# Ten value tiles and six feature tiles moved between the last blocks of the first modulation, five of its blocks left unsplit

## What is computed

```python
mod = silu(cond) @ w_mod + b_mod            # shift1, scale1, gate1, shift2, scale2, gate2
h   = x * (1 + scale1) + shift1
z   = h @ w_in                              # q, k, v of 8 heads, and the latents of the second attention
# ... two attentions, w_o, layer norm
x   = layernorm(alpha * x + gate1 * o)
x   = layernorm(alpha * x + gate2 * swiglu(x * (1 + scale2) + shift2))
```

## Time and profile before

| | us |
|---|---|
| median of 3 runs (2892.14 to 2893.25) | 2892.49 |
| the profiled execution | 2892.7 |
| its span in the trace | 2891.1 |
| first modulation: first matmul, start of block 63 on PE | 7.73, 91.50 |
| first matmul of value block 0 | 99.62 |
| first matmul behind the value blocks | 215.12 |

### The profile page before, as it was taken

One profiled execution on the slowest core, in us unless ns is written; L12 is line 12 of the kernel. 1 busy time (PEld: TensorE's weight loads), 2 busy tenths in 40 slices (PEclk: granted clock), 3 DMA queues, 4 the chain that ended last, 5 costly groups with the idle time before them and its releaser, 6 DMA issues.

```text
span 2891.1 us, 42097 instructions
## 1 busy us (share of the span) xinstructions
PE 2814.6 (97%) x15844; PEld 2494.9 (86%) x15844; DVE 1889.6 (65%) x2939; ACT 1043.8 (36%) x1814; POOL 187.9 (6%) x262
## 2 busy tenths in 40 slices
PE   7899999999999999799999999999999999999996
PEld 2679999877888776799999999999999888888885
DVE  8766666585885787866666666666666555424337
ACT  7422333224453213644444444444444312112121
POOL 1121111000001000000000000000000000000005
PEclk9999999999999999899999999999999999999998
DMA  9754333352334655122222222222222535223231
GB/s 383 274 186 154 125 128 132 122 191 71 104 110 173 220 175 182 63 101 97 101 101 101 99 98 101 101 99 92 96 101 101 198 119 174 80 89 137 80 124 73
DMA packets 105768, 379.82 MB, mean 131 GB/s; under 512 B 14062, under 2 KB 14466, under 8 KB 103754
## 3 DMA queue, kind: packets, MB, share of 16 engines
q1 hardware_dynamic: 89088, 317.36, 30.9%
q0 software_dynamic: 16000, 61.06, 6.0%
q10 hardware_dynamic: 586, 0.12, 0.0%
HBM read 346.97 MB, written 33.48 MB: 132 GB/s over the span
## 4 chain that ended last, share of the span: by engine, by line
PE 90%; DVE 4%; DMA 2%; ACT 2%; issue 1%; SPq 0%; ACTq 0%; DVEq 0%
PE ps L1955 16%; PE ps L1957 16%; PE ps L1956 16%; PE ps L2455 12%; PE ps L2453 12%; PE ps L2454 12%; DMA mraw<-in_wstream 2%; PE ps L2154 1%; PE ps L2119 1%; DVE ps L1883 1%; PE ps L2102 1%; DVE acc L1885 1%; DVE stat L1933 0%; PE ps L2150 0%; PE ps L2093 0%
## 5 line engine op out<-in xcount | busy, mean ns | idle before, releaser
L2453 PE MATMUL ps<-actl,ringh 128*128 128x320 f32 x1408 | 435.5, 309 | 3.9 <-DVE ringl L1754 3.9
L2454 PE MATMUL ps<-acth,ringh 128*128 128x320 f32 x1408 | 435.1, 309 | 0.0
L2455 PE MATMUL ps<-actl,ringl 128*128 128x320 f32 x1408 | 435.1, 309 | 0.0
L2453 PE MATMUL ps<-acth,ringh 128*128 128x320 f32 x1056 | 327.1, 310 | 7.6 <-DVE ringl L1754 7.6
L2454 PE MATMUL ps<-actl,ringh 128*128 128x320 f32 x1056 | 326.9, 310 | 0.0
L2455 PE MATMUL ps<-acth,ringl 128*128 128x320 f32 x1056 | 326.8, 309 | 0.0
L1955 PE MATMUL ps<-dwh,fring 128*128 128x512 f32 x820 | 319.4, 390 | 1.0 <-DVE dwl L1858 1.0
L1957 PE MATMUL ps<-dwh,fring 128*128 128x512 f32 x820 | 319.2, 389 | 0.0
L1956 PE MATMUL ps<-dwl,fring 128*128 128x512 f32 x820 | 319.1, 389 | 0.0
L1858 DVE TENSOR_TENSOR dwl<-raw,dwh 128x1024 fp32r<-128x1024 f32 x82 | 100.4, 1224 | 291.4 <-ACT dwh L1319 291.4
L1754 DVE TENSOR_TENSOR ringl<-raw,ringh 128x512 fp32r<-128x512 f32 x264 | 181.7, 689 | 162.8 <-ACT ringh L1253 162.8
(11 more groups left out here) (310 smaller groups left out, 5775.0 us busy)
## 6 DMA issues: line engine op xcount, KB each, us to landing
raw<-in_wstream SPq DMA_DIRECT2D x503, 512.0 KB, 3.3
mraw<-in_wstream SPq DMA_DIRECT2D x64, 512.0 KB, 7.7
fscr<-fst POOLq DMA_DIRECT2D x44, 320.0 KB, 2.4
fst<-fscr SPq DMA_DIRECT2D x21, 640.0 KB, 4.1
acc<-in_xT SPq DMA_DIRECT2D x8, 640.0 KB, 16.0
oscr<-ost POOLq DMA_DIRECT2D x16, 320.0 KB, 2.5
ostage<-oscr POOLq DMA_DIRECT2D x16, 320.0 KB, 3.9
acc<-in_xtok POOLq DMA_DIRECT2D x4, 1280.0 KB, 7.4
```

The lines of the kernel that those rows point to most:

```text
L2453: mm(out, ringh[:, s, w], ah, start=first, stop=False, skip_group_check=True)
L2454: mm(out, ringh[:, s, w], al, start=False, stop=False, skip_group_check=True)
L2455: ins = mm(out, ringl[:, s, w], ah, start=False, stop=last, skip_group_check=True)
```

## The change

Between the last blocks of the modulation PE now computes value blocks 0 and 1, one value tile (six matmuls) behind each of the blocks 49, 50, 52, 54, 55 and 57, 58, 60, 62, 63. For this the feature tiles 0 to 5 are made between the splits of ACT and DVE, behind the blocks 43, 45, 48, 51, 56 and 60 (`H_AT`), value blocks 0 to 2 are split behind 47, 53 and 59 (`V_SPLIT`), and `mod1` is made in three parts. SP loads x 0, 1, 2 behind the blocks 36, 42 and 50 (`X_LOAD`) and the value blocks 0 to 3 behind 39, 46, 54 and 61 (`V_LOAD`). The blocks 44, 46, 50, 54 and 58 (`DIRECT`) aren't split: PE multiplies them as they are, with both operands in plain float32, in two matmuls in place of four. `modrow` has one buffer in place of two, the loops over the blocks are written out, and `mraw` and a few small buffers lie elsewhere in SBUF, so that feature tiles 0 to 5 don't overlap the blocks that are still in use. The product of block 2 is behind block 63, with the last `turn_rows` behind its first tile. What follows value block 2 is in the order of before.

The core of the diff:

```diff
+DIRECT = [44, 46, 50, 54, 58]
+SPLIT = [j for j in range(B_V) if j not in DIRECT]
+X_LOAD = {36: 0, 42: 1, 50: 2}
+V_LOAD = {39: 0, 46: 1, 54: 2, 61: 3}
+V_SPLIT = {47: 0, 53: 1, 59: 2}
+V_TILES = {49 + 8 * v + x: (v, t) for v in range(2) for t, x in enumerate((0, 1, 3, 5, 6))}
+H_AT = {43: 0, 45: 1, 48: 2, 51: 3, 56: 4, 60: 5}
+def mod_row(j):
+    return j
+def pe_order():
+    order = []
+    for j in range(B_V):
+        order.append(mod_row(j))
+        if j in V_TILES and V_TILES[j][1] == 4:
+            order.append(B_V + V_TILES[j][0])
+    return order
+PE_ORDER = pe_order()
...
+SPLITS = [n for k, n in ORDER if k == "w"]
+RAWS = [(k, n) for k, n in ORDER if k == "m" or n >= B_V]
+RAW_POS = {x: B_V + p for p, x in enumerate(RAWS)}
+RAW_END = B_V + len(RAWS)
...
-        MOD_BANKS = [7, 5]
+        MOD_BANKS = [4, 5]
...
-            for n in range(8):
-                sp.dma_start(mraw[:, n, :], wstream[n]).then_inc(mod_loaded[n], 16)
-            with sp.Fori(1, B_V // 8) as i:
-                for s in range(8):
-                    sp.wait_ge(lo_ready, i * 8 + (s - 7))
-                    sp.dma_start(mraw[:, s, :], wstream[i * 8 + s]).then_inc(mod_loaded[s], 16)
-            for g in range(8):
+            def mod_load(j):
+                if j - 8 in DIRECT:
+                    sp.wait_ge(used, used_count(mod_row(j - 8)))
+                elif j >= 8:
+                    sp.wait_ge(lo_ready, POS[("w", mod_row(j - 8))] + 1)
+                sp.dma_start(mraw[j % 8], wstream[mod_row(j)]).then_inc(mod_loaded[j % 8], 16)
+            def stream_load(p):
+                if p >= B_V + 4:
+                    sp.wait_ge(lo_ready, POS[RAWS[p - 4 - B_V]] + 1)
+                sp.dma_start(raw[:, p % 4, :], wstream[stream_row(p)]).then_inc(loaded[p % 4], 16)
+            for j in range(B_V):
+                mod_load(j)
+                if j in X_LOAD:
+                    g = X_LOAD[j]
+                    sp.dma_start(xstage[:, 2 * g:2 * g + 2, :], xT[:, 2 * g:2 * g + 2, :]).then_inc(x_in[g], 16)
+                if j in V_LOAD:
+                    stream_load(B_V + V_LOAD[j])
+            for g in range(3, 8):
                 sp.dma_start(xstage[:, 2 * g:2 * g + 2, :], xT[:, 2 * g:2 * g + 2, :]).then_inc(x_in[g], 16)
-                if g < 4:
-                    sp.dma_start(raw[:, g, :], wstream[stream_row(B_V + g)]).then_inc(loaded[g], 16)
-            def stream_load(p):
-                sp.wait_ge(lo_ready, p - 3)
-                sp.dma_start(raw[:, p % 4, :], wstream[stream_row(p)]).then_inc(loaded[p % 4], 16)
-            for p in range(B_V + 4, len(ORDER)):
+                if g in (4, 6):
+                    stream_load(B_V + 2 + g // 2)
+            for p in range(B_V + 6, RAW_END):
                 stream_load(p)
...
-            def mod_split(i, n):
-                act.wait_ge(mod_loaded[n % 8], at(i, 32, 16 * (n // 8 + 1)))
-                if i is not None or n >= 4:
-                    act.wait_ge(used, at(i, 16, n - 3))
-                nc.scalar.activation(mhi[:, n % 4, :], mraw[:, n % 8, :], ACT.Copy).then_inc(hi_ready, 1)
...
+            def mod_split(j):
+                x = SPLIT.index(j)
+                act.wait_ge(mod_loaded[j % 8], 16 * (j // 8 + 1))
+                if x >= 4:
+                    act.wait_ge(used, used_count(mod_row(SPLIT[x - 4])))
+                nc.scalar.activation(mhi[:, x % 4, :], mraw[j % 8], ACT.Copy).then_inc(hi_ready, 1)
+            def mod_rows(c):
+                act.wait_ge(used, used_count(mod_row(8 * c + 7)))
+                if c:
+                    act.wait_ge(mod1_psum, c)
+                nc.scalar.activation(modrow[:, :], ps[MOD_BANKS[c % 2]][0:4, :], ACT.Copy).then_inc(modrow_ready, 1)
             def h_part(k):
                 act.wait_ge(h_scaled, k + 1)
                 nc.scalar.activation(hh[:, k, :], pb[:, k % 3, :], ACT.Copy).then_inc(h_hi, 1)
-            for b in range(16):
+            for j in range(B_V):
+                if j not in DIRECT:
+                    mod_split(j)
+                if j % 8 == 3 and j >= 8:
+                    mod_rows(j // 8 - 1)
+                if j in V_SPLIT:
+                    split(None, B_V + V_SPLIT[j])
+                if j in H_AT:
+                    h_part(H_AT[j])
+            mod_rows(7)
+            h_part(6)
+            split(None, B_V + 3)
+            h_part(7)
+            for b in range(2, 16):
                 if b < 6:
-                    for k in (range(6) if b == 0 else range(2 * b + 4, 2 * b + 6)):
+                    for k in range(2 * b + 4, 2 * b + 6):
                         h_part(k)
-                        if b == 0 and k == 1:
-                            split(None, B_V + 1)
...
-            def mod_split(i, n):
-                dve.wait_ge(hi_ready, at(i, 16, n + 1))
-                V.tensor_tensor(mlo[:, n % 4, :], mraw[:, n % 8, :], mhi[:, n % 4, :].bitcast(f32),
+            def mod_split(j):
+                x = SPLIT.index(j)
+                dve.wait_ge(hi_ready, SPLITS.index(mod_row(j)) + 1)
+                V.tensor_tensor(mlo[:, x % 4, :], mraw[j % 8], mhi[:, x % 4, :].bitcast(f32),
                                 ALU.subtract).then_inc(lo_ready, 1)
-            for n in range(16):
-                mod_split(None, n)
-            with dve.Fori(1, 4) as i:
-                for n in range(16):
-                    mod_split(i, n)
-            split(None, B_V)
-            dve.wait_ge(mod1_psum, 8)
-            dve.wait_ge(consts_in, 16 * CONSTS)
             psum1 = ps[6][:, 0:4 * KD].rearrange("p (k c) -> p k c", c=2)
             bc = bcols[:, :].unsqueeze(2).to_broadcast([P, 2 * KD, 2])
             bc2 = bcols2[:, :].unsqueeze(2).to_broadcast([P, 2 * KD, 2])
-            V.tensor_tensor(mod1[:, 0:KD, :], psum1[:, 0:KD, :], bc[:, 0:KD, :], ALU.add)
-            own.link(V.scalar_tensor_tensor(out=mod1[:, KD:2 * KD, :], in0=psum1[:, KD:2 * KD, :], scalar=1.0,
-                                            in1=bc[:, KD:2 * KD, :], op0=ALU.add, op1=ALU.add))
+            def mod1_part(q):
+                dve.wait_ge(mod1_psum, 8 if q == 2 else q + 5)
+                if q == 0:
+                    dve.wait_ge(consts_in, 16 * CONSTS)
+                end = q + 1 if q < 2 else 4
+                k = slice(4 * q, 4 * end)
+                V.tensor_tensor(mod1[:, k, :], psum1[:, k, :], bc[:, k, :], ALU.add)
+                k = slice(KD + 4 * q, KD + 4 * end)
+                V.scalar_tensor_tensor(out=mod1[:, k, :], in0=psum1[:, k, :], scalar=1.0, in1=bc[:, k, :],
+                                       op0=ALU.add, op1=ALU.add).then_inc(mod1_ready, 1)
             def h_part(k):
                 dve.wait_ge(x_in[k // 2], 16)
+                if k in (0, 4, 8):
+                    dve.wait_ge(mod1_ready, k // 4 + 1)
                 if k >= 3:
                     dve.wait_ge(h_ready, k - 2)
...
-            for b in range(16):
+            for j in range(B_V):
+                if j not in DIRECT:
+                    mod_split(j)
+                if j in V_SPLIT:
+                    split(None, B_V + V_SPLIT[j])
+                if j in (43, 52):
+                    mod1_part(j // 9 - 4)
+                if j in H_AT:
+                    h_part(H_AT[j])
+                if j - 1 in H_AT:
+                    h_rest(H_AT[j - 1])
+            h_part(6)
+            h_part(7)
+            h_rest(6)
+            mod1_part(2)
+            split(None, B_V + 3)
+            h_part(8)
+            h_rest(7)
+            for b in range(2, 16):
                 if b < 6:
-                    ks = list(range(6) if b == 0 else range(2 * b + 4, 2 * b + 6))
-                    if b == 0:
-                        h_part(0)
-                    for k in ks:
+                    for k in range(2 * b + 4, 2 * b + 6):
                         if k + 1 < KD:
                             h_part(k + 1)
                         h_rest(k)
-                        if b == 0 and k == 1:
-                            split(None, B_V + 1)
...
-            def mod_block(i, n, b, chunk_free, bank, hi, lo):
-                pe.wait_ge(lo_ready, at(i, 16, n + 1))
-                if b == 0 and chunk_free is not None:
-                    pe.wait_ge(modrow_ready, chunk_free)
+            def mod_block(j):
+                c, b = divmod(j, 8)
+                bank = MOD_BANKS[c % 2]
+                if b == 0 and c >= 2:
+                    pe.wait_ge(modrow_ready, c - 1)
+                if j in DIRECT:
+                    pe.wait_ge(mod_loaded[j % 8], 16 * (j // 8 + 1))
+                else:
+                    pe.wait_ge(lo_ready, POS[("w", mod_row(j))] + 1)
                 for kk in range(2):
                     w = slice(kk * 512, (kk + 1) * 512)
-                    mm(ps[bank][0:4, :], condw[:, 2 * b + kk, :], hi[:, w], start=(b == 0 and kk == 0), stop=False)
```

(41 more changed lines are left out.)

76 lines of the change are left out of this document (32 added, 44 removed).

## The result

| | before | after |
|---|---|---|
| median of 20 runs each (lowest to highest), us | 2892.69 (2890.41 to 2896.56) | 2897.95 (2895.07 to 2899.39) |
| ratio, 95% interval | | 1.0016 [1.001, 1.0022] |
| profiled execution, its span | 2892.7, 2891.1 | 2899.39, 2897.8 |
| start of the heads' projection (end of the value blocks) | 215.12 | 222.18 |
| from there to the end of the span | 2676.0 | 2675.6 |

The changed kernel is 5.3 us slower, 0.16%, which is just inside the 0.2% that were called "the same", though the interval leaves out no change at all. 2896.0 was forecast and the range held the time. But the number is that of rival 2 (2897.7), not of the case that was held to be the likeliest, and the profile shows that rival 2 is what happened.

The account below looks back on a forecast made before the run. PE, busy 97% of the span, was taken as the bound, with DMA bounding the first modulation. Block 49 at 84.8, plus 32.6 and 101.0, gave 218.4 against 215.12; taken as +3.5: 2896.0 us, range 2890.3 to 2900.0.

Parts of the forecast that it names:

- rival 2: Idle time ahead of block 49 brings half clock onto full work: 1.7 us lost, +5.2, 2897.7 us; chance 22%.
- the case that was held to be the likeliest: The forecast: PE starts block 49 at 84.8, heads' projection at 218.4, +3.5 us, 2896.0 us; chance 48%.
- What bounds the kernel, loads: In the first modulation DMA is full at 409 to 410 GB/s; loads put ahead bring block 43 4.48 us later.
- The hand-overs: Ahead of block 49, ACT and DVE handing three feature tiles over between splits cost 5.3 us: 84.8, not 79.5.
- Rival 1: Hand-overs don't bind; PE reaches block 49 at the loads' pace, 79.5: -1.8 us, 2890.7 us; chance 10%.
- The price of an unsplit block: An unsplit block on PE takes 1.8 us, as the row sums, against 0.93 split; 5.4 us for 50, 54, 58.
- The work left: PE's work without waits: 32.6 us from block 49 through block 63's tile, then 101.0 to the heads' projection.
- Rival 3: Hand-overs go on to bind behind block 49, PE waits 3.1 us: +6.6, 2899.1 us; chance 15%.
- Value block 3: Behind block 63, its tiles 6 and 7 are ready at 123.3, PE has work until 125.4: hidden, 2 us margin.
- Behind the stage: After the value blocks the engines keep the order of before, so the 3.5 us shift passes through to the end.

Follow-up runs that it names:

- e_loads: The kernel before with only SP's loads put in the changed kernel's order, no tile moved: 2902.2 us, ratio 1.0033 to the kernel before.
- e_lag: The changed kernel with ACT's rounding and DVE's rest of feature tiles 0 to 5 one split later: 2893.46 us, 1.0003 of the kernel before.
- e_direct2: The changed kernel with only blocks 44 and 46 unsplit, and 50, 54 and 58 split: 2896.49 us, 1.0014 of the kernel before.
- e_chunks: The changed kernel with modulation chunks ordered 0, 4, 1, 5, 2, 6, 3, 7, another table throughout, blocks 19, 20, 22, 42 unsplit: 2880.68 us.

## Why the prediction was right, and where it was not

- **What bounds the kernel, loads:** right. ACT takes block 43 at 68.46 (68.2 was said), with DMA at 1.03 and 409 GB/s. e_loads shows the whole price of the loads, 10.5 us at the first value matmul.
- **The hand-overs:** right in place and size. PE starts block 49 at 85.28 (84.8); e_lag moves it to 82.59. Rival 1, 79.5, is out. But of the 5.3 us that the prediction put down to the hand-overs only 3.2 are theirs (e_lag). The other 2.1 stay when they are gone; which of the splits and tiles on the two engines hold them was not separated.
- **The price of an unsplit block:** right, 1.81 us from the row sums. It was used for three blocks that bring nothing, as e_direct2 shows.
- **The work left:** right. From 121.01 to 222.18 are 101.2 us (101.0 was said). From block 49 to 121.01 are 35.7 us against 32.6. The 3.1 are the 2.9 of the clock and 0.2 of small things.
- **The step that failed** is the choice between the forecast and rival 2. The prediction described rival 2 rightly ("PE would be busy for 0.9 of the 3.8 us ahead of block 49", a like stretch at half clock behind it, full work in it) and gave it 22%, though its own numbers (0.9 of 3.8 busy, with 1.5 of 3.4 followed by half clock in the earlier trace rows) made it, in hindsight, the likelier case. (Idle time isn't always followed by half clock, as 63.79 to 67.20 shows, so rival 2 was no certainty.) Its size was too small as well: 1.7 us, from a stretch of 3.4; it was 6.8 long and cost 2.9. The nearest place of the kernel before had that length, 95.90 to 102.70 behind a stretch with 1.10 of 3.4 us busy, and the prediction had its price (8.5 in place of 7.0 us) and used it only as something that goes away. That the median is within 0.3 us of rival 2's number is luck: in the profiled execution the heads come 1.9 us later than rival 2 has them (215.12 + 5.2 = 220.3), and the median lies 1.4 us below that execution, for a reason that the one trace doesn't show.
- **Rival 3**, hand-overs that bind behind block 49, did not occur: PE is busy for all of the 136.9 us from 85.28 to the heads' projection, and even with three more splits it waits for only 0.46 us (e_direct2).
- **Value block 3** was hidden as said: DVE ends `hl` of tile 7 at 126.4, PE needs it at 129.2, four tiles of 1.4 behind the turn's end at 123.5.
- **Behind the stage** the shift was handed through, 2675.6 against 2676.0, but that this is exact to half a microsecond was luck, as the next section but one shows.

## What to carry to other kernels

Work that is to fill another stage's waits needs its operands early, and these come over the very resource that bounds the stage: write down first what that costs (here 10.5 us), and then how much of the waits lies where the work can already exist (in the changed kernel 4 us; in e_chunks the tiles leave PE no idle time from 63 on). Two engines that hand a tile to and fro should do the second half one step later than the first, and a wait of TensorE just ahead of dense work is to be priced with the time at half clock behind it, not only with itself.
